# Order of VectorE's work inside one step of the eight-head attentions

## The chip, the cores and the metric

One core of one Trainium2 chip runs the whole program in a single launch. The metric is the device time of that core in microseconds; the kernel before took 3082.2 us (median of three runs, 3080.27 to 3089.55). The engines work from queues of their own, in the order in which the program gave them their instructions, and meet only at semaphores: TensorE (PE) multiplies, turns tiles (transposes) and fills the eight banks of PSUM, ScalarE (ACT) and VectorE (DVE) read these banks, GpSimd (POOL) works in SBUF, SyncE (SP) issues transfers.

## The reference, cut to what matters

1024 tokens of width 1024 pass two layers of a first kind and two of a second kind. A layer of the first kind projects its input, runs a differential attention of four heads with a bias by relative position, runs an attention of eight query heads on two key and value heads, and projects out. A layer of the second kind has a gating unit, an indexer that selects up to 256 keys for each query, and an attention of eight query heads on one key head over the selected, causal keys. The eight-head attentions, cut short:

```python
def gqa_attention(q, k, v):            # first kind: every key, 8 heads on 2
    sc = einsum('bgrqd,bgkd->bgrqk', qblk * d ** -0.5, kt)
    p = softmax(sc, axis=-1)
    return einsum('bgrqk,bgkd->bgrqd', p, vt)

def sparse_attention(...):             # second kind: 8 heads on 1, causal and selected
    sc = where(valid, einsum('bthd,btkd->bthk', qb, k_sel) * attn_scale, -inf)
    p = softmax(sc, axis=-1)
    return einsum('bthk,btkd->bthd', p, v_sel)
```

All of it is in float32. The kernel gets this accuracy from TensorE's faster format by cutting each operand of a product in two: a high part, which is the value rounded to that format, and a low part, which is the value less its high part. A product is then the sum of two or three products of such parts.

## The kernel before, in words

`heads_phase` computes one eight-head attention. It is called once per layer, four times in all: with the tag `b_` in the two layers of the first kind, and with the tag `x_` in the two layers of the second kind, where it is causal.

Its unit of work is a **row**: 128 queries of one head against their keys, a tile of 128 partitions by up to 1024 elements. There are 64 rows in a call, numbered g = 0 to 63: four pairs of heads, in each pair eight blocks of 128 queries, in each block first the one head and then the other. In the `b_` calls every row has 1024 keys. In the `x_` calls a row has 128 keys for the first block of queries, 256 for the second and so on up to 1024, and then the next pair of heads begins with 128 again; the selection comes in as the `bias` that is added.

The life of a row is: TensorE multiplies its scores into PSUM (`scores`, L1111, two rows at a time, in banks 0 to 3). VectorE adds the bias or zero, negates, writes the row to SBUF and keeps the maximum (`shift`, L970). ScalarE takes the exponential in place and keeps the sum (`exponent`, L906). VectorE takes the reciprocal of the sum (`invert`, L978). GpSimd scales the row by it (L1034). When four rows of one head are ready, TensorE turns them: a **turned tile** is 128 keys by 512 queries, made of up to four transposes (`turn`, L1072), in one of the banks 4 to 6. ScalarE copies the high part out (`take` of the scalar program, L890), VectorE the low part, which is the bank less the high part (`take` of the vector program, L953), and TensorE multiplies both by the values (`product`, L1089 and L1090). After the last tile of a group ScalarE reads the result (`close`, L897 and L900) and GpSimd gates it (L1006, L1011).

Every engine has its own program, and each program is a loop over the same steps g = START to END, here from -5 to 78. A table called `plan` says which tiles are turned in which step. In the `b_` calls it is two tiles in each of the steps 8 to 71; in the `x_` calls it is one or two, of 128 to 512 columns. The queries and keys of the next pair of heads are turned by the same table ("stack" tiles, L1066, L882, L945), one more tile in each of a few steps. What the engines issue in step g is this:

- TensorE: the products of the tiles of `plan[g-2]`; if g is odd, the scores of rows g+1 and g+2, which wait until row g has been shifted; then the turns of `plan[g]`.
- ScalarE: the high parts of `plan[g-1]`; every fourth step a `close`; then the exponential of row g, which waits for the shift of row g.
- VectorE: the shift of row g, which waits for its scores; the reciprocal of row g-1; then the low parts of `plan[g-1]`, each of which waits for its high part.
- GpSimd: the scaling of row g-1, and every fourth step two operations of 64 by 512.

Nothing reorders these queues: an instruction that waits holds up all that its engine was given later. In the `b_` calls the last steps of the four-head attention before it are interleaved with steps -5 to 14 (`next(before)`), so that this attention's rows overlap the end of the other one.

Of the kernel before, what the change touches and what calls it, by code (L numbers as in the profile page):

```python
# [721 lines left out]
def heads_phase(nc, env, tag, groups, queries, group_of, y_of, bias=None, load=(), ahead=(), gating=(), host=None):  # L722
# [13 lines left out]
    def query_tile(g):  # L736
        return g % (2 * T) // 2
# [13 lines left out]
    def group_with(g):  # L751
        return 2 * (g // 8) + g % 2
# [10 lines left out]
    def tile_lo(n, j):  # L763
        return max(0, j - QB * half_of(n)) * P if causal else 0
# [9 lines left out]
    plan = {g: [] for g in range(START, END + 1)}  # L774
    for z, (_, at) in enumerate(stacks):
        plan[at].append(("stack", z, 0))
        plan[at if at < 0 else at + 1].append(("stack", z, 1))
# [8 lines left out]
    last_tile = [number["attn", n, tiles(n) - 1] + 1 for n in range(NSB)]  # L786
    last_rank = [rank["attn", n, tiles(n) - 1] + 1 for n in range(NSB)]
    stack_of = {what: z for z, (what, _) in enumerate(stacks)}

    with ExitStack() as c:  # L790
# [36 lines left out]
        def stack(z):  # L827
            what, i = stacks[z][0]
            return key_st[i][:, :, :] if what == "k" else query_st[i % 2][:, :, :]

        def scale_of(z):
            return 1.0 if stacks[z][0][0] == "k" else HD ** -0.5

        def bank(e):
            return 4 + number[e] % (2 if host and number[e] < 4 else 3)

        def score_view(g):
            pair = 2 * (g % 2)
            kn = keys(g)
            if kn > BANK:  # L840
                return ps[:, pair:pair + 2, 0:kn // 2]
            return ps[:, pair, 0:kn]

        def row_view(row, g):
            kn = keys(g)
            return row.rearrange("p (b n) -> p b n", b=2) if kn > BANK else row

        def prob(g):
            return pr[g % RING]

        with Phase(nc, joins=host.ph if host else None, continued=True) as ph:
# [8 lines left out]
            @ph.sync  # L860
            def _(sp):
                if host:
                    sp.wait_ge(host.y_done, host.blocks)
                for dst, src in load:
                    sp.dma_start(dst, src).then_inc(y_in, 16)
                for dst, src, sem in ahead:
                    sp.dma_start(dst, src).then_inc(sem, 16)

            @ph.block.scalar
            def _(act):  # L870
                def take(e):
                    act.wait_ge(turned, number[e] + 1)
                    if e[0] == "stack":
                        _, z, side = e
                        what, p = stacks[z][0]
                        if what == "q" and p >= 2:
                            act.wait_ge(scored, T * (p - 1))
                        if host and z < 2:
                            act.wait_ge(host.shifted, 2 * (host.rows - T))
                        elif host:  # L880
                            act.wait_ge(host.pv_done, host.products)
                        nc.scalar.activation(stack(z)[:, 0, side * BANK:(side + 1) * BANK], ps[:, bank(e), :], ACT.Copy,  # L882
                                             scale=scale_of(z)).then_inc(stk_hi, 1)
                        return
                    kk, lo = rank[e], tile_lo(e[1], e[2])
                    if kk >= SLOTS:
                        act.wait_ge(pv_done, kk - SLOTS + 1)
                    elif host:
                        act.wait_ge(host.pv_done, host.products)
                    nc.scalar.activation(ath[:, kk % SLOTS, lo:], ps[:, bank(e), lo:], ACT.Copy).then_inc(th_done, 1)  # L890
# [47 lines left out]
            @ph.block.vector  # L938
            def _(dve):
                def take(e):  # L940
                    if e[0] == "stack":
                        _, z, side = e
                        cols = slice(side * BANK, (side + 1) * BANK)
                        dve.wait_ge(stk_hi, moved[e])
                        nc.vector.scalar_tensor_tensor(stack(z)[:, 1, cols], ps[:, bank(e), :], scale_of(z),  # L945
                                                       stack(z)[:, 0, cols].bitcast(F32), ALU.mult,
                                                       ALU.subtract).then_inc(stk_lo, 1)
                        return
                    kk, lo = rank[e], tile_lo(e[1], e[2])
                    dve.wait_ge(th_done, kk + 1)  # L950
                    if kk >= SLOTS:
                        dve.wait_ge(pv_done, kk - SLOTS + 1)
                    nc.vector.tensor_tensor(atl[:, kk % SLOTS, lo:], ps[:, bank(e), lo:],  # L953
                                            ath[:, kk % SLOTS, lo:].bitcast(F32), ALU.subtract).then_inc(tl_done, 1)

                def shift(g):
                    dve.wait_ge(scored, g // 2 + 1)
                    if g >= NS:
                        dve.wait_ge(exped, g - NS + 1)
                    if g >= RING:  # L960
                        dve.wait_ge(turned, last_tile[group_with(g - RING)])
                    elif host and g == 0:
                        dve.wait_ge(host.scored, host.rows)
                    elif host and g == 5:
                        dve.wait_ge(host.combined, host.rows)
                    elif host and g == 8:
                        dve.wait_ge(host.turned, host.turns)
                    added = (row_view(bias(query_tile(g)), g) if causal
                             else zero.unsqueeze(2).broadcast_to([P, 2, BANK]))
                    nc.vector.tensor_tensor_reduce(out=row_view(prob(g), g), in0=score_view(g), in1=added,  # L970
                                                   scale=-1.0, scalar=3.0e38, op0=ALU.add, op1=ALU.min,
                                                   accum_out=nm[:, g % NS:g % NS + 1]).then_inc(shifted, 1)

                def invert(g):
                    dve.wait_ge(exped, g + 1)
                    if g >= NS:
                        dve.wait_ge(normed, g - NS + 1)
                    nc.vector.reciprocal(rr[:, g % NS:g % NS + 1], sums[:, g % NS:g % NS + 1]).then_inc(recip, 1)  # L978

                before = steps[1](dve)  # L980
                if not causal:
                    nc.vector.memset(zero, 0.0).then_inc(zeroed, 1)
                    dve.wait_ge(zeroed, 1)
                for _ in range(alone):
                    next(before)
                for g in range(START, END + 1):
                    next(before, None)
                    if 0 <= g < NB:
                        shift(g)
                    if 1 <= g <= NB:  # L990
                        invert(g - 1)
                    for e in plan.get(g - 1, []):
                        take(e)
                    for i in range(NG):
                        if g == split_step[i]:
                            dve.wait_ge(v_hi, i + 1)
                            nc.vector.tensor_tensor(vv[i][:, :, HD:], groups[i][1],
                                                    vv[i][:, :, 0:HD].bitcast(F32), ALU.subtract).then_inc(v_lo, 1)
# [1687 lines left out]
```

## Time and profile before

| | before |
|---|---|
| median of three runs | 3082.2 us |
| the profiled execution | 3083.09 us |
| its span | 3081.2 us |
| its mean granted TensorE clock | 0.937 of full speed |
| PE / DVE / ACT / POOL busy | 2690.7 / 2030.6 / 1566.3 / 1155.1 us |

The page also cuts the span into 40 equal slices of about 77 us; a digit is the busy share of a slice in tenths. The first shift of the two `b_` calls starts at 542.5 and 1375.2 us of the span, that of the two `x_` calls at 2123.0 and 2812.6 us; the last one follows some 190 us later in a `b_` call and some 134 us later in an `x_` call. Below, times on the left of a timeline row are microseconds from the span's start.

### The profile page before, as it was taken

How to read it: one execution, taken by the hardware profiler on the slowest of the kernel's cores; microseconds unless marked ns; L12 is line 12 of the kernel's file. 1: busy time of each engine (PE TensorE's matmuls, PEld its weight loads, DVE VectorE, ACT ScalarE, POOL GpSimd, SP SyncE). 2: the span in 40 equal slices, each digit the busy share in tenths (PEclk: the TensorE clock that was granted, in tenths of full speed). 3: DMA queues.
4: the chain of work that ended last, by engine and by line, in shares of the span. 5: the costliest groups of instructions: out<-in, count | busy, mean ns of one | idle time of the engine just before them, and what ended most of it. 6: DMA issues, size and time to landing. Idle time of an engine off the chain costs nothing. (4 is left out here: it accounts for less than half of the span.)

```text
span 3081.2 us, 41522 instructions
## 1 busy us (share of the span) xinstructions
PE 2690.7 (87%) x14032; PEld 2114.1 (69%) x14032; DVE 2030.6 (66%) x4318; ACT 1566.3 (51%) x3035; POOL 1155.1 (37%) x981
## 2 busy tenths in 40 slices
PE   6999888898979997989989796997889697997887
PEld 5877666676868775656777585776667575776666
DVE  4472487798434724877974348997767358997766
ACT  3221276788423113757873216684764316684751
POOL 0100277564001003765630002984741002984731
PEclk9999899999989998999999899998999898998999
DMA  4443210101324421001022101110032100110022
GB/s 124 118 140 99 91 40 8 42 1 43 109 70 130 141 81 56 20 8 42 1 95 91 55 21 28 45 45 25 1 123 76 58 18 28 45 45 25 1 89 82
DMA packets 90750, 181.93 MB, mean 59 GB/s; under 512 B 12552, under 2 KB 27912, under 8 KB 90504
## 3 DMA queue, kind: packets, MB, share of 16 engines
q1 hardware_dynamic: 74124, 150.69, 15.4%
q10 hardware_dynamic: 16416, 28.61, 3.1%
q8 instruction: 111, 1.82, 0.3%
q14 instruction: 99, 0.81, 0.1%
HBM read 149.87 MB, written 33.33 MB: 59 GB/s over the span
## 5 line engine op out<-in xcount | busy, mean ns | idle before, releaser
L1362 POOL TENSOR_SCALAR a_prob<-a_prob,a_ratio 128x1024 f32<-128x1024 f32 x64 | 72.1, 1127 | 515.8 <-DVE a_ratio L1321 515.8
L718 PE MATMUL ps<-w_hi,hh 128*128 128x512 f32 (+1 forms) x640 | 242.4, 379 | 22.2 <-DVE w_lo L603 10.1
L718 PE MATMUL ps<-w_lo,hh 128*128 128x512 f32 (+1 forms) x640 | 240.0, 375 | 0.0
L718 PE MATMUL ps<-w_hi,hl 128*128 128x512 f32 (+1 forms) x640 | 239.9, 375 | 0.0
L1801 PE MATMUL ps<-o_w_hi,hh 128*128 128x512 f32 x512 | 212.5, 415 | 24.3 <-DVE o_w_lo L1725 24.3
L2263 DVE TENSOR_SCALAR_CACHE_REDUCE select_rows<-masks,select_cuts 128x1024 bf16<-128x1024 int16 (+7 forms) x264 | 230.2, 875 | 0.2
L1801 PE MATMUL ps<-o_w_lo,hh 128*128 128x512 f32 x512 | 207.6, 405 | 0.0
L1801 PE MATMUL ps<-o_w_hi,hl 128*128 128x512 f32 x512 | 206.7, 404 | 0.0
L1781 POOL TENSOR_TENSOR o_rstd<-o_rstd,nhalf 128x1 f32<-128x1 f32 x56 | 46.7, 835 | 409.6 <-DVE o_rstd L1662 235.3
L1034 POOL TENSOR_SCALAR b_prob<-b_prob,a_guest_small 128x1024 f32<-128x1024 f32 x128 | 144.6, 1129 | 127.6 <-DVE a_guest_small L978 124.9
L1310 DVE CUSTOM_DVE_ANT_0 a_prob<-ps,a_bias 128x1024 f32<-128x1024 f32 x128 | 151.7, 1222 | 59.5 <-PE ps L1452 55.0
L970 DVE CUSTOM_DVE_ANT_1 b_prob<-ps,a_guest_small 128x1024 f32<-128x1024 f32 x128 | 156.1, 1219 | 31.3 <-PE ps L1111 31.3
L953 DVE TENSOR_TENSOR a_attn_t_lo<-ps,a_attn_t_hi 128x512 fp32r<-128x512 f32 x256 | 163.7, 681 | 14.2 <-ACT a_attn_t_hi L890 13.7
L906 ACT ACTIVATE b_prob<-b_prob,a_guest_small 128x1024 f32<-128x1024 f32 x128 | 147.6, 1154 | 30.5 <-DVE a_guest_small L970 30.2
L2437 PE MATMUL ps<-hh,w_hi 128*128 128x512 f32 x384 | 153.7, 400 | 10.6 <-ACT y L2187 7.6
L890 ACT ACTIVATE a_attn_t_hi<-ps 128x512 fp32r<-128x512 f32 x256 | 139.4, 599 | 35.6 <-PE ps L1072 34.7
L718 PEld LDWEIGHTS ps<-w_hi,hh 128*128 128x128 f32 x640 | 121.7, 190 | 52.0 <-DVE w_lo L603 20.6
L539 ACT ACTIVATE w_hi<-w_raw 128x512 fp32r<-128x512 f32 (+1 forms) x56 | 33.7, 601 | 240.9 <-PE ps L718 229.4
L2079 PE MATMUL ps<-w_hi,hh 128*128 128x512 f32 (+1 forms) x384 | 140.0, 365 | 17.6 <-DVE w_lo L2047 12.6
L1265 ACT ACTIVATE a_prob<-a_prob,a_neg_max 128x1024 f32<-128x1024 f32 x128 | 146.0, 1148 | 17.8 <-DVE a_neg_max L1310 17.5
L1365 POOL TENSOR_TENSOR a_prob<-a_prob 128x1024 f32<-128x1024 f32 x64 | 152.7, 2386 | 5.3
L2437 PE MATMUL ps<-hl,w_hi 128*128 128x512 f32 x384 | 152.8, 398 | 0.0
(356 smaller groups left out, 7914.8 us busy)
## 6 DMA issues: line engine op xcount, KB each, us to landing
w_early<-in_w_in SPq DMA_DIRECT2D x108, 256.0 KB, 2.8
ada_w<-in_w_ada ACTq DMA_DIRECT2D x96, 256.0 KB, 2.7
w_raw<-in_w_in SPq DMA_DIRECT2D x84, 256.0 KB, 2.7
ak<-gates SPq DMA_DIRECT2D x32, 256.0 KB, 3.7
xcur<-aq SPq DMA_DIRECT2D x16, 512.0 KB, 3.6
y<-xcur SPq DMA_DIRECT2D x16, 512.0 KB, 3.8
a_bias<-bias_tiles SPq DMA_DIRECT2D x8, 960.0 KB, 4.9
bq<-in_w_out SPq DMA_DIRECT2D x12, 512.0 KB, 4.0
```

Source lines behind the costliest of these rows:

```text
L718: mm = nc.tensor.matmul(o, lhs, rhs, start=(k == 0 and i == 0), stop=(k == K - 1 and i == 2))
L906: nc.scalar.activation(prob(g), prob(g), ACT.Exp, bias=nm[:, g % NS:g % NS + 1], scale=-1.0, accum_out=sums[:, g % NS:g % NS + 1]).then_in ...
L953: nc.vector.tensor_tensor(atl[:, kk % SLOTS, lo:], ps[:, bank(e), lo:], ath[:, kk % SLOTS, lo:].bitcast(F32), ALU.subtract).then_inc(tl_do ...
L970: nc.vector.tensor_tensor_reduce(out=row_view(prob(g), g), in0=score_view(g), in1=added, scale=-1.0, scalar=3.0e38, op0=ALU.add, op1=ALU.m ...
L1034: nc.gpsimd.tensor_scalar(prob(b), prob(b), rr[:, b % NS:b % NS + 1], 0.5, ALU.mult, ALU.mult).then_inc(normed, 1)
L1265: nc.scalar.activation(row, row, ACT.Exp, bias=nm[:, g % NS, m:m + 1], scale=-1.0, accum_out=out).then_inc(exped, 1)
L1310: nc.vector.tensor_tensor_reduce(out=row, in0=scores_of(g, m), in1=bias, scale=-1.0, scalar=3.0e38, op0=ALU.add, op1=ALU.min, accum_out=nm ...
L1365: nc.gpsimd.tensor_tensor(row0(g), row0(g), row1(g), ALU.add).then_inc(combined, 1)
L1801: mm = nc.tensor.matmul(o, lhs, rhs, start=(k == 0 and i == 0), stop=(k == K - 1 and i == 2))
L2079: mm = nc.tensor.matmul(ps[:, b, 0:n], lhs, rhs, start=(k == 0 and i == 0), stop=(k == K - 1 and i == 2))
L2263: spare_free[z] = mark(nc.vector.tensor_scalar(spare[:, z, 0:(qb + 1) * P], values, against, None, op, ALU.add, accum_out=column(count_of, ...
L2437: mm = nc.tensor.matmul(ps[:, b, :], lhs, rhs, start=(k == 0 and i == 0), stop=(k == K - 1 and i == 2))
```

## The change

In each step of the loop of the vector program of `heads_phase`, the low parts of the turned tiles of `plan[g-1]` are issued before the shift of row g and the reciprocal of row g-1, and no longer behind them. No instruction is added, removed or resized, and the programs of the other engines stay as they are. It applies to all four calls.

```diff
@@ -985,12 +985,12 @@
                     next(before)
                 for g in range(START, END + 1):
                     next(before, None)
+                    for e in plan.get(g - 1, []):
+                        take(e)
                     if 0 <= g < NB:
                         shift(g)
                     if 1 <= g <= NB:
                         invert(g - 1)
-                    for e in plan.get(g - 1, []):
-                        take(e)
                     for i in range(NG):
                         if g == split_step[i]:
                             dve.wait_ge(v_hi, i + 1)
```

## Rows read from the trace of the kernel before

**Rows 1.** The page, part 1: engine, busy us, share, instructions.

```profile
PE 2690.7 (87%) x14032; PEld 2114.1 (69%) x14032; DVE 2030.6 (66%) x4318; ACT 1566.3 (51%) x3035; POOL 1155.1 (37%) x981
```

**Rows 2.** Windows: shift 8 to shift 63 of each call, busy us by engine, clock.

```profile
576.00:733.00 157.00, 152.18 (x1010) 116.42 (x1011) 141.02 (x283) 139.73 (x253) 97.19 (x87) 0.99 0.06 21
1408.70:1565.70 157.00, 152.33 (x1011) 116.51 (x1011) 141.08 (x284) 139.68 (x253) 97.35 (x87) 0.99 0.06 21
2133.90:2257.40 123.50, 104.88 (x665) 80.91 (x665) 89.50 (x250) 96.40 (x219) 93.36 (x96) 0.90 0.00 1
2823.50:2946.70 123.20, 104.57 (x665) 80.96 (x665) 89.61 (x249) 96.53 (x219) 93.30 (x96) 0.90 0.00 1
```

**Rows 3.** Waits of 576 to 733 us: us in total, times, longest.

```profile
DVE b_prob L970 <- PE ps L1111: 14.6, 27, 1.9
...
DVE a_attn_t_lo L953 <- ACT a_attn_t_hi L890: 1.1, 5, 0.2
```

**Rows 4.** Timeline, a few steps of a b_ call: start us, us, engine, line.

```profile
652.96 1.09 ACT L890 ACTIVATE a_attn_t_hi<-ps 128x512 fp32r<-128x512 f32 x2
...
653.59 1.29 DVE L953 TENSOR_TENSOR a_attn_t_lo<-ps,a_attn_t_hi 128x512 fp32r<-128x512 f32 x2 [0.21 <-ACT a_attn_t_hi L890]
...
653.93 1.16 ACT L906 ACTIVATE b_prob<-b_prob,a_guest_small 128x1024 f32<-128x1024 f32 x1
...
654.79 1.22 DVE L970 CUSTOM_DVE_ANT_1 b_prob<-ps,a_guest_small 128x1024 f32<-128x1024 f32 x1
...
655.06 1.09 ACT L890 ACTIVATE a_attn_t_hi<-ps 128x512 fp32r<-128x512 f32 x2
...
656.05 1.18 ACT L906 ACTIVATE b_prob<-b_prob,a_guest_small 128x1024 f32<-128x1024 f32 x1
...
656.07 1.66 PE L1111 MATMUL ps<-b_key_stack,b_query_stack 64*128 64x512 f32 x12 [0.16 <-DVE a_guest_small L970]
...
657.66 1.09 PE L1072 MATMUL ps<-ident,b_prob 128*128 128x128 f32 x8
...
658.36 1.09 ACT L890 ACTIVATE a_attn_t_hi<-ps 128x512 fp32r<-128x512 f32 x2 [1.04 <-PE ps L1072]
```

**Rows 5.** Windows of an x_ call around a fall of the clock.

```profile
2185.00:2190.00 5.00, 3.08 (x19) 2.07 (x19) 4.08 (x15) 4.19 (x11) 4.82 (x5) 0.87 0.01 2
2190.00:2195.00 5.00, 5.00 (x25) 4.56 (x24) 2.46 (x6) 3.86 (x8) 2.33 (x4) 0.50 0.01 3
```

**Rows 6.** Windows around one in a b_ call, the same columns.

```profile
570.00:575.00 5.00, 3.73 (x24) 2.87 (x24) 2.58 (x8) 3.43 (x6) 2.72 (x3) 0.92 0.00 0
575.00:580.00 5.00, 5.00 (x28) 3.46 (x26) 3.58 (x8) 2.73 (x6) 4.70 (x8) 0.74 0.00 0
```

**Rows 7.** Timeline, work of TensorE at the lower clock, and what follows it.

```profile
573.56 2.40 PE L1111 MATMUL ps<-b_key_stack,b_query_stack 64*128 64x512 f32 x12
...
576.00 1.23 DVE L970 CUSTOM_DVE_ANT_1 b_prob<-ps,a_guest_small 128x1024 f32<-128x1024 f32 x1 [1.90 <-PE ps L1111]
...
2189.47 1.94 PE L1072 MATMUL ps<-ident,x_prob 128*128 128x128 f32 x8 [0.51 <-DVE x_attn_t_lo L953]
...
2192.72 0.43 DVE L970 CUSTOM_DVE_ANT_0 x_prob<-ps,masks 128x256 f32<-128x256 f32 x1
```

**Rows 8.** Groups by line, 2133.9 to 2257.3 us: busy us, mean ns, idle.

```profile
L906 ACT ACTIVATE x_prob<-x_prob,x_neg_max 128x640 f32<-128x640 f32 (+7 forms) x55 | 43.9, 798 | 7.0 <-DVE x_neg_max L970 6.8
L970 DVE CUSTOM_DVE_ANT_0 x_prob<-ps,masks 128x640 f32<-128x640 f32 (+7 forms) x55 | 43.1, 783 | 15.2 <-PE ps L1111 15.2
L953 DVE TENSOR_TENSOR x_attn_t_lo<-ps,x_attn_t_hi 128x512 fp32r<-128x512 f32 (+1 forms) x78 | 41.1, 549 | 14.8 <-ACT x_attn_t_hi L890 14.2
L890 ACT ACTIVATE x_attn_t_hi<-ps 128x512 fp32r<-128x512 f32 (+1 forms) x78 | 35.8, 486 | 19.8 <-PE ps L1072 19.5
```

**Rows 9.** Timeline, scores of two narrow rows of an x_ call and what follows.

```profile
2191.66 1.01 PE L1111 MATMUL ps<-x_key_stack,x_query_stack 64*128 64x256 f32 x6
...
2192.60 0.69 PE L1072 MATMUL ps<-ident,x_prob 128*128 128x128 f32 x2
```

**Rows 10.** Timeline, scores of two wide rows of an x_ call and what follows.

```profile
2253.90 1.66 PE L1111 MATMUL ps<-x_key_stack,x_query_stack 64*128 64x512 f32 x12 [0.57 <-DVE x_neg_max L970]
2255.49 0.55 PE L1072 MATMUL ps<-ident,x_prob 128*128 128x128 f32 x3
```

## The prediction

> **What bounds the kernel now.** I read the engine totals first, then the four calls of `heads_phase` one by one. TensorE is busy 2690.7 of 3081.2 us [rows 1], so most of the kernel follows it, but inside the calls two or three engines are nearly full together. Between the shift of row 8 and that of row 63, a `b_` call takes 157.0 us: TensorE is busy 152.2, VectorE 141.0, ScalarE 139.7. An `x_` call takes 123.5 and 123.2 us, with TensorE at 105 and VectorE at 90 [rows 2]. These stretches are the ones that the change touches, 55 shifts each, with turned tiles in every step. The waits say what is late in a `b_` call: VectorE waits 14.6 us in 27 pieces for scores, which is once in two rows, and only 1.1 us for high parts [rows 3]. So VectorE runs shift, reciprocal, two low parts, and meets a high part that has almost always been copied. The timeline shows why that is so: while VectorE shifts row g (654.79), ScalarE has gone on from the exponential of the row before (653.93) to the two high copies (655.06), and the low parts come only after the shift. High copies and shift lie side by side. That is the slack to watch.
>
> **The change, part by part.** Nothing is added or taken away, so what has to be found is which waits get a new place. Write S(g) for the shift, E(g) for the exponential, H(g) for the high parts of the tiles of `plan[g-1]` and L(g) for their low parts. ScalarE issues H(g), E(g), H(g+1), E(g+1). VectorE issued S(g), L(g), S(g+1), L(g+1) and now issues L(g), S(g), L(g+1), S(g+1). As a cyclic order that looks the same, a low part between any two shifts, but it is another low part: L(g+1) now stands between S(g) and S(g+1), where L(g) stood. L(g+1) needs H(g+1). ScalarE has this behind E(g), and E(g) waits for S(g). So every row now closes a serial chain: S(g), E(g), H(g+1), L(g+1), S(g+1). Before, H(g+1) had the whole of S(g+1) as cover. Behind the waiting low part on VectorE stand the next shift and the reciprocal, behind these TensorE's next scores, ScalarE's next exponential and GpSimd's scaling, so no engine can run ahead of the ring.
>
> The price of one turn of this ring in a `b_` call, start to start [rows 4]: shift to exponential 654.79 to 656.05, 1.26; exponential to first high copy 653.93 to 655.06, 1.13; first high copy to first low part 652.96 to 653.59, 0.63 (VectorE had waited 0.21 for it, so that is the true delay); two low parts to the next shift 653.59 to 654.79, 1.20. Sum 4.22 us. This holds for a shift of odd g.
>
> For even g a second chain is longer, because the scores of row g are issued before the turns of `plan[g-1]` and wait for S(g-1): shift to scores 654.79 to 656.07, 1.28; scores to turns 656.07 to 657.66, 1.59; turns to high copy 657.66 to 658.36, 0.70; then again 0.63 and 1.20. Sum 5.40 us [rows 4]. Before, the scores alone stood between these two shifts and the turns were hidden.
>
> From shift 8 to shift 63 there are 28 links of the odd kind and 27 of the even kind: 28 x 4.22 = 118.2 and 27 x 5.40 = 145.8. Eight stack tiles fall in these steps, each with one more low part of about 0.60 (half of 1.20): 4.8. Together 268.8 us against 157.0 [rows 2], so **+112 us** per `b_` call with TensorE's clock unchanged.
>
> In an `x_` call the terms are the group means [rows 8]. Shift 0.783 and 0.05 until the next engine starts (as 1.22 stands to 1.26 and 1.28 in rows 4): 0.83. Exponential 0.82. High copy 0.486 + 0.03: 0.52. Low parts 0.549 less the 0.08 by which the next one overlaps, 0.47 each, with 78 tiles in 55 steps 1.42 of them: 0.67. An odd link is 2.84. An even link replaces the exponential by scores and turns. Wide scores take 1.59 from start to start [rows 10]; narrow ones took 0.94 at the lower clock [rows 9], say 0.54 at the full one; over the eight widths I take 1.00, and 0.62 for the turns, which are often fewer than four: 3.64. 28 x 2.84 + 27 x 3.64 = 177.8, and six stack tiles at 0.6 make 181.4, against 123.5 [rows 2]: **+58 us**.
>
> **The clock.** TensorE's work for two rows of a `b_` call is at most 152.2 / 27.5 = 5.5 us. In a ring of 4.22 + 5.40 = 9.6 us it has all of it ready early (turns and products follow the scores), so about 4.1 us in each 9.6 us are idle and in one piece. In the trace, 3.08 us of work in 5 us, in pieces, was followed by a granted clock of 0.50, which is 1.2 GHz; so it was, less deep, in the `b_` call at 575 us [rows 5, 6]. A stretch with TensorE nearly full kept 0.99 of 2.4 GHz [rows 2]. I expect the clock to fall in most of these idle pieces and to come back during the work behind them, and then it is the scores and the first turns that run at half speed, and these are on the ring. Priced: scores across part of a fall took 2.44 us (573.56 to 576.00), as against 1.59, and at most 2 x 1.59 = 3.18; I take 2.8. From the start of slow turns to the next shift it was 3.25 (2189.47 to 2192.72) as against 0.70 + 0.63 + 1.20 = 2.53 [rows 7]. An even link at the low clock is 1.28 + 2.8 + 3.25 = 7.33, which is 1.93 more. All 27 of them would add 52 us, none of them nothing. I take two thirds, +35. In the `x_` calls the scores are 1.00 and not 1.59, so the surcharge is some 1.2 us, 33 us for all; these calls are at 0.90 already and have less in one piece, so I take half, +16.
>
> On this the Trainium skill has a rule that speaks against me: TensorE: Matmul & The Clock Gate, section "Loop structure matters more than you think", says that a copy out of PSUM by VectorE between groups of matmuls does not cost TensorE its warm clock, and that it is long waits for transfers that do. Its example has the next matmuls follow at once. By it the surcharge of the paragraph above would be nothing. The trace at 2185 to 2195 us, with no transfer to wait for (DMA share 0.01), had the clock fall to 0.50, so here the row and the broad reading of the rule differ.
>
> **What is moved past.** The reciprocal of row g-1 now comes a low part later. GpSimd waits for it, but has 97 busy us in 157 [rows 2] and now 1.7 times the time; a group's first turn needs its last row two steps on. I cost it at nothing; if that cover were gone, it would be the 1.2 us of two low parts in one step of four. The low parts of the last rows are issued no earlier than before, so the tails behind shift 63 and the steps below 9, which have no tiles of this phase but stacks ahead of row 0, cost nothing either. No DMA is moved, and no queue of SP or GpSimd.
>
> **Sum.** A `b_` call: 112 + 35 = +147. An `x_` call: 58 + 16 = +74. Two of each: +442. The profiled execution took 3083.1, 0.9 above the median of 3082.2, so both give some **3525 us**, 14% more.
>
> **The rivals.**
> - The clock stays at 2.4 GHz in the rings. Only 2 x (112 + 58) = +340: 3422 us. For it speaks that `b_` calls hold 0.99 today; against it the idle of 4.1 us in one piece.
> - The clock is low in every even link: 2 x (112 + 52 + 58 + 33) = +510, 3592 us. For it: the idle piece repeats at every second row. Against: the work behind it is long enough that the clock rises again, and a late, slow piece of work makes the next idle piece shorter.
> - The other side, faster. If ScalarE had the high parts ready when VectorE starts a step, the low parts would fill VectorE's wait for scores (14.6 us in a `b_` call, 15.2 in an `x_` call [rows 3, 8]) and free banks and products a step earlier; at best 2 x (14.6 + 15.2) = -60, 3023 us. It decides if H(g) is issued ahead of the wait for S(g-1) on ScalarE. It is not: the code puts E(g-1), which waits for that shift, in front of it.
> - The change does less than it says: the ring binds only for even g, as if the odd one were hidden in work that the ring leaves over. A row takes 157.0 / 55 = 2.85 us today. Then per `b_` call 27 x (5.40 - 2.85) = 69, and in proportion (58 / 112) 36 per `x_` call: +210, 3293 us. But an odd link of 4.22 is above 2.85 too, and its four terms wait for each other, so nothing can hide it.
>
> **How the numbers follow.** The forecast (some even links slow) gets 0.55, the low clock everywhere 0.25, the full clock 0.14, the half ring 0.03, the faster case with no change 0.03. The range goes from the full clock to the low clock with 5 us per call for waits that my sums leave out: 3420 to 3610; what is left out is the half ring and the other side, and a little of each end. Apart from no change one can tell about 0.3%, 9 us; every slower case is far beyond: slower 0.97, same 0.02, faster 0.01.
>
> **What would show it.** In the changed kernel, VectorE should wait for high parts (L953 on L890) instead of for scores, in nearly every step: some 2 us each time, (269 - 141) / 55 = 2.3 in a `b_` call. In a timeline the order should be shift, exponential, high copies, low parts, shift with no overlap, 4.2 us from an even row to the odd one and 5.4 to 7.3 from an odd row to the even one. ScalarE's and VectorE's busy times must not move. The clock of a `b_` call should be below 0.99, near 0.8. If VectorE's waits for high parts stay near 1 us per call, my reading of ScalarE's order is wrong; if the clock is 0.99 and the time near 3422, only the surcharge is.

## The result

| | before | changed |
|---|---|---|
| median | 3085.9 us (3080.3 to 3091.2, 4 runs) | 3546.4 us (3533.7 to 3549.8, 4 runs) |
| ratio, with its 95% interval | | 1.149 [1.146, 1.152] |
| span of the profiled execution | 3081.2 us | 3532.0 us |
| mean granted TensorE clock | 0.937 | 0.891 |

The change made the kernel 460 us slower; 3525 had been forecast.

The page of the changed kernel, part 1, engine, busy us, share and instructions:

```profile
PE 2822.2 (80%) x14032; PEld 2218.5 (63%) x14032; DVE 2035.5 (58%) x4318; ACT 1584.6 (45%) x3035; POOL 1151.5 (33%) x981
```

Against [rows 1], VectorE's and ScalarE's work has hardly moved (+5 and +18 us). TensorE has gained 132 busy us with the same instructions: part of them run at the lower clock. The windows of the changed kernel from shift 8 to shift 63 of its four calls, columns as in [rows 2] (start and end, length, busy us of TensorE, its weight loads, VectorE, ScalarE and GpSimd, then clock, DMA share and GB/s):

```profile
574.70:884.40 309.70, 201.95 (x1023) 154.83 (x1023) 145.50 (x285) 146.98 (x256) 97.14 (x87) 0.80 0.03 11
1557.70:1867.50 309.80, 201.99 (x1022) 154.75 (x1023) 145.48 (x285) 146.97 (x256) 97.20 (x87) 0.80 0.03 11
2434.50:2634.70 200.20, 129.06 (x668) 100.64 (x668) 88.76 (x250) 100.77 (x221) 95.02 (x97) 0.76 0.00 1
3197.70:3398.50 200.80, 126.53 (x668) 98.96 (x668) 88.52 (x250) 100.56 (x221) 95.00 (x97) 0.76 0.00 1
```

157.0 us have become 309.7 and 309.8, and 123.5 and 123.2 have become 200.2 and 200.8: 460 us in these four stretches, against 451 in the span. The other 9 us were gained back outside them and were not traced further. (The profiled execution was the fastest of the four; the medians differ by 460 us.) The clock fell from 0.99 to 0.80 and from 0.90 to 0.76. Waits of the first stretch, us in total, times, longest, against [rows 3]:

```profile
DVE a_attn_t_lo L953 <- ACT a_attn_t_hi L890: 143.6, 60, 4.6
PE ps L1111 <- DVE a_guest_small L970: 106.5, 27, 4.5
...
ACT b_prob L906 <- DVE a_guest_small L970: 94.6, 55, 2.5
ACT a_attn_t_hi L890 <- PE ps L1072: 60.9, 39, 2.8
...
DVE b_prob L970 <- PE ps L1111: 1.9, 1, 1.9
```

VectorE's wait for high parts went from 1.1 to 143.6 us. Its shifts wait 1.9 us for scores, no longer 14.6: the scores are now ready, because VectorE is late. One turn of the chain in the changed kernel's timeline, start and duration in us:

```profile
769.08 1.22 DVE L970 CUSTOM_DVE_ANT_1 b_prob<-ps,a_guest_small 128x1024 f32<-128x1024 f32 x1
...
770.34 1.15 ACT L906 ACTIVATE b_prob<-b_prob,a_guest_small 128x1024 f32<-128x1024 f32 x1 [1.90 <-DVE a_guest_small L970]
...
771.49 1.06 ACT L890 ACTIVATE a_attn_t_hi<-ps 128x512 fp32r<-128x512 f32 x2
772.09 1.29 DVE L953 TENSOR_TENSOR a_attn_t_lo<-ps,a_attn_t_hi 128x512 fp32r<-128x512 f32 x2 [1.72 <-ACT a_attn_t_hi L890]
773.30 1.22 DVE L970 CUSTOM_DVE_ANT_1 b_prob<-ps,a_guest_small 128x1024 f32<-128x1024 f32 x1
...
774.58 2.93 PE L1111 MATMUL ps<-b_key_stack,b_query_stack 64*128 64x512 f32 x12 [4.05 <-DVE a_guest_small L970]
...
777.44 1.21 PE L1072 MATMUL ps<-ident,b_prob 128*128 128x128 f32 x8
778.25 1.09 ACT L890 ACTIVATE a_attn_t_hi<-ps 128x512 fp32r<-128x512 f32 x2 [2.45 <-PE ps L1072]
...
778.88 1.29 DVE L953 TENSOR_TENSOR a_attn_t_lo<-ps,a_attn_t_hi 128x512 fp32r<-128x512 f32 x2 [4.28 <-ACT a_attn_t_hi L890]
...
780.09 1.21 DVE L970 CUSTOM_DVE_ANT_1 b_prob<-ps,a_guest_small 128x1024 f32<-128x1024 f32 x1
```

Each step of this path starts when the one before it lets it: shift, exponential, high parts, low parts, shift takes 4.22 us (769.08 to 773.30). Then shift, scores, turns, high, low, shift takes 6.79 us; TensorE had stood idle for 4.05 us, and its scores take 2.86 (774.58 to 777.44) and not 1.59.

### The profile page after: what moved, and what is told of

Its sections match the earlier page's. It is cut to its first block and busy times, and to the rows that moved or that the text cites. A ratio compares the mean times of both kernels' runs of the same rounds, so it can differ in the third digit from the quotient of the medians.

```text
span 3532.0 us, 41522 instructions
## 1 busy us (share of the span) xinstructions
PE 2822.2 (80%) x14032; PEld 2218.5 (63%) x14032; DVE 2035.5 (58%) x4318; ACT 1584.6 (45%) x3035; POOL 1151.5 (33%) x981
## 3 DMA queue, kind: packets, MB, share of 16 engines
q8 instruction: 111, 1.82, 0.2%
## 5 line engine op out<-in xcount | busy, mean ns | idle before, releaser
L1111 PE MATMUL ps<-b_key_stack,b_query_stack 64*128 64x512 f32 x768 | 159.7, 569 | 217.3 <-DVE a_guest_small L970 217.3
L1111 PEld LDWEIGHTS ps<-b_key_stack,b_query_stack 64*128 64x128 f32 x768 | 99.0, 266 | 262.3 <-DVE a_guest_small L970 216.6
L718 PE MATMUL ps<-w_hi,hh 128*128 128x512 f32 (+1 forms) x640 | 242.7, 379 | 22.2 <-DVE w_lo L603 10.1
L953 DVE TENSOR_TENSOR x_attn_t_lo<-ps,x_attn_t_hi 128x512 fp32r<-128x512 f32 x192 | 102.5, 555 | 208.8 <-ACT x_attn_t_hi L890 208.4
L1111 PE MATMUL ps<-x_key_stack,x_query_stack 64*128 64x512 f32 (+4 forms) x576 | 99.4, 486 | 151.3 <-DVE x_neg_max L970 148.4
L1034 POOL TENSOR_SCALAR x_prob<-x_prob,x_recip 128x256 f32<-128x256 f32 (+7 forms) x128 | 95.4, 746 | 271.5 <-DVE x_recip L978 271.1
L1111 PEld LDWEIGHTS ps<-x_key_stack,x_query_stack 64*128 64x128 f32 x576 | 66.5, 262 | 174.9 <-DVE x_neg_max L970 143.1
L1072 PEld LDWEIGHTS ps<-ident,b_prob 128*128 128x128 f32 x1024 | 145.0, 168 | 48.6 <-issue 34.9
L1072 PE MATMUL ps<-ident,b_prob 128*128 128x128 f32 x1024 | 169.8, 319 | 6.6 <-DVE a_attn_t_lo L953 3.5
```

The costliest lines, as they stand in the source:

```text
L718: mm = nc.tensor.matmul(o, lhs, rhs, start=(k == 0 and i == 0), stop=(k == K - 1 and i == 2))
L1034: nc.gpsimd.tensor_scalar(prob(b), prob(b), rr[:, b % NS:b % NS + 1], 0.5, ALU.mult, ALU.mult).then_inc(normed, 1)
L1072: mm = nc.tensor.transpose(ps[:, bank(e), i * P:(i + 1) * P], prob(rows_in(n)[i])[:, j * P:(j + 1) * P], ident[:, :])
L1111: mm = nc.tensor.matmul(ps[:, 2 * m + b, 0:w], q_st[rows, qe, tok], k_st[rows, ke, cols], start=(i == 0), stop=(i == 2))
```

## The experiments

"Odd link" is the time from the start of an even shift to the next, odd one; "even link" from an odd shift to the even one behind it. Spans of calls run from shift 8 to shift 63. Each ratio is to runs of the kernel before on the same chip (medians 3080 to 3084 us).

**x_calls_only.** The change in the `x_` calls alone.

```diff
+                    for e in lows if causal else []: take(e)
                     shift(g); invert(g - 1)
+                    for e in [] if causal else lows: take(e)
```

> The new order in the two x_ calls alone; the b_ calls keep the old one. If each call pays for its own serial chain and nothing passes between them, the two x_ calls grow by 77 us each, as in the changed kernel, and the b_ calls stay at 157 us from shift 8 to shift 63: 3086 + 154 = 3240 us, within 10. If part of the loss of the changed kernel came from elsewhere (the clock carried over, a later start of the next phase), the two parts would not add up and this kernel would lie over 20 us away from 3240.

Measured 3236.3 us, 1.051 [1.047, 1.054]. The first `b_` call takes 157.0 us as before, the `x_` calls 200.9 and 202.3. Each call pays for itself and the parts add up.

**warm_filler.** The changed kernel with work for TensorE in its idle pieces.

```diff
+ if not causal and g % 2 and 11 <= g < NB:   # PE, ahead of the scores
+     for i in range(24): transpose(bank of the next turn, ident, ident)
```

> The changed kernel, with 24 transposes of the identity added in each odd step of the b_ calls, into a bank that the next turns overwrite, in the idle piece of TensorE ahead of the scores (24 x 0.11 = 2.6 us at the full clock, idle piece about 4.1 us). If the low clock is what makes an odd-to-even link 6.9 us and not 5.40, the clock stays near 1.0 in the b_ calls, these links fall to 5.4 and the odd ones stay at 4.22: 309.7 - 40 = 270 us a call, 3546 - 80 = 3466 us. If the 5.40 was simply too low and the clock costs nothing, the links stay at 6.9 and the time at 3546, or goes above it by what the filler delays.

Measured 3478.3 us, 1.129 [1.124, 1.134]; the `b_` calls take 278.1 and 275.7 us, the `x_` calls, which have no filler, 202.3 and 200.7. Window of the first `b_` call, and a piece of its timeline (the filler is L1123, the added line has moved the others by one):

```profile
570.20:848.30 278.10, 231.58 (x1667) 196.65 (x1668) 143.99 (x285) 145.30 (x256) 97.89 (x87) 0.97 0.04 12
```

```profile
702.35 1.22 DVE L971 CUSTOM_DVE_ANT_1 b_prob<-ps,a_guest_small 128x1024 f32<-128x1024 f32 x1
...
703.63 1.66 PE L1112 MATMUL ps<-b_key_stack,b_query_stack 64*128 64x512 f32 x12 [1.60 <-DVE a_guest_small L971]
...
705.22 1.09 PE L1073 MATMUL ps<-ident,b_prob 128*128 128x128 f32 x8
705.91 1.09 ACT L891 ACTIVATE a_attn_t_hi<-ps 128x512 fp32r<-128x512 f32 x2 [1.05 <-PE ps L1073]
...
707.75 1.22 DVE L971 CUSTOM_DVE_ANT_1 b_prob<-ps,a_guest_small 128x1024 f32<-128x1024 f32 x1
...
708.88 2.78 PE L1123 MATMUL ps<-ident 128*128 128x128 f32 x24
```

With useless work in the gap the clock is 0.97, and the even link is 5.40 (702.35 to 707.75), the sum of the prediction to the hundredth; 22 of the 27 even links of this call lie between 5.38 and 5.49. More work for TensorE made the kernel 68 us faster by the medians, and the two `b_` calls together 66. They are 8 and 6 us above the 270 expected: five even links of the first call take 6.4 to 9.0, one of them before the filler begins and two with scores that start only 3.38 us after the shift, behind the filler.

**exp_behind_high.** The changed kernel, ScalarE's exponential one step later.

```diff
-                    if 0 <= g < NB: exponent(g)
+                    if 1 <= g <= NB: exponent(g - 1)
```

> The changed kernel, with ScalarE's exponential of a row one step later, so behind the high parts of that step: H(g), E(g-1), H(g+1), E(g). If the odd link of 4.22 is the chain shift, exponential, high part, low part, the exponential now leaves it: the link falls to what VectorE needs, 1.20 + 0.08 + 1.22, 2.5 to 2.9 us; the even link keeps scores and turns, 5.4 at the full clock and up to 7.3. A b_ call 28 x 2.6 + 27 x 5.4 to 6.9 + 5 = 224 to 264, an x_ call about 150 to 170: 3270 to 3390 us. If ScalarE's order is not on the path (the loss is the late reciprocal, or VectorE's own order), nothing changes: 3546 us.

Measured 3324.2 us, 1.079 [1.075, 1.083]; calls 235.7, 236.2, 163.8, 165.7 us. An odd link and the even link behind it:

```profile
702.70 1.22 DVE L970 CUSTOM_DVE_ANT_1 b_prob<-ps,a_guest_small 128x1024 f32<-128x1024 f32 x1
...
703.92 1.27 DVE L953 TENSOR_TENSOR a_attn_t_lo<-ps,a_attn_t_hi 128x512 fp32r<-128x512 f32 x2
...
705.10 1.22 DVE L970 CUSTOM_DVE_ANT_1 b_prob<-ps,a_guest_small 128x1024 f32<-128x1024 f32 x1
...
706.38 1.66 PE L1111 MATMUL ps<-b_key_stack,b_query_stack 64*128 64x512 f32 x12 [2.06 <-DVE a_guest_small L970]
...
710.50 1.22 DVE L970 CUSTOM_DVE_ANT_1 b_prob<-ps,a_guest_small 128x1024 f32<-128x1024 f32 x1
```

Odd links fall from 4.22 to 2.40, which is VectorE's own work. Even links in a `b_` call are 5.4 at least (705.10 to 710.50) and 6.1 in the mean, with the clock at 0.90. So the exponential is on the odd link and not on the even one.

**turns_before_scores.** The changed kernel, TensorE's turns of an odd step ahead of its scores.

```diff
+                    if g % 2: turns of plan[g]
                     if g % 2: scores(g + 1)
-                    turns of plan[g]
+                    if g % 2 == 0: turns of plan[g]
```

> The changed kernel, with TensorE's turns of an odd step ahead of the scores of that step. If the even link is shift, scores, turns, high part, low part, the turns leave it and the chain through the exponential is left for both kinds: 55 x 4.22 + 5 = 237 us for a b_ call, and here the low clock costs little (shift 1.28 and slow scores 2.8 to 2.93 are 4.2 together, as long as the other chain). An x_ call 55 x 2.84 + 4 = 160. 3086 + 2 x (80 + 37) = 3320 us, 3300 to 3350. If the turns are not on the path, 3546.

Measured 3347.6 us, 1.087 [1.084, 1.090]; calls 244.0, 242.2, 171.0, 168.0 us. Even links go from 6.98 in the mean to between 4.22 and 4.38 in 23 of 27 steps, and most odd ones stay at 4.22. What is left on an even link is the chain through the exponential:

```profile
704.35 1.22 DVE L970 CUSTOM_DVE_ANT_1 b_prob<-ps,a_guest_small 128x1024 f32<-128x1024 f32 x1
...
705.61 1.15 ACT L906 ACTIVATE b_prob<-b_prob,a_guest_small 128x1024 f32<-128x1024 f32 x1 [0.92 <-DVE a_guest_small L970]
...
706.88 1.09 ACT L890 ACTIVATE a_attn_t_hi<-ps 128x512 fp32r<-128x512 f32 x2
...
707.51 1.29 DVE L953 TENSOR_TENSOR a_attn_t_lo<-ps,a_attn_t_hi 128x512 fp32r<-128x512 f32 x2 [1.86 <-ACT a_attn_t_hi L890]
...
708.71 1.21 DVE L970 CUSTOM_DVE_ANT_1 b_prob<-ps,a_guest_small 128x1024 f32<-128x1024 f32 x1
```

The time lies at the upper end of what was expected: the `x_` calls take 8 to 11 us more than the 160 that the group means gave, and a few steps with a third tile take up to 7.6.

**one_low_first.** Half of the change: of two low parts the first ahead of the shift.

```diff
+                    for e in lows[:len(lows) // 2]: take(e)
                     shift(g); invert(g - 1)
+                    for e in lows[len(lows) // 2:]: take(e)
```

> The new order for half of the tiles only: in a step with two turned tiles the first low part stands ahead of the shift and the second behind; a single tile is taken behind, as before. If the terms of the chain add up, a b_ call's links are each one low part (0.60) shorter than in the changed kernel: 3.62 and 6.3 (6.9 with the clock's part, less 0.60), 28 x 3.62 + 27 x 6.3 + 3 = 274 us. An x_ call has two tiles in half of its steps: about 160. 3086 + 2 x (117 + 37) = 3390 us, 3360 to 3420. If only the number of low parts ahead of the shift counted, half of the loss: 3316.

Measured 3307.6 us, 1.072 [1.069, 1.074]: 82 us below what was expected, outside its range, and near the 3316 of the other reading, half of the loss. The total can't tell the two apart; the links do. Odd links are 3.62 and the shortest even ones 4.80, each 0.60 less than with two, as expected. What failed is, for some 47 us, the clock's part: I had kept all of it (6.3), and the mean is 5.5 in the `b_` calls, 250.3 and 250.9 us. Window of the first:

```profile
572.20:822.40 250.20, 183.87 (x1018) 135.59 (x1018) 142.46 (x284) 146.62 (x256) 97.75 (x87) 0.89 0.04 13
```

A shorter link leaves a shorter idle piece, and the clock is 0.89 instead of 0.80. The other 36 us are the `x_` calls, in which single tiles have no ring here: 142.0 and 141.6 us, not 160.

**reciprocal_last.** The kernel before, with the reciprocal behind the low parts.

```diff
                     shift(g)
+                    low parts of plan[g - 1]
                     invert(g - 1)
-                    low parts of plan[g - 1]
```

> The kernel before, with the reciprocal of the last row behind the low parts and not between shift and low parts: shift, low parts, reciprocal. It is the only other thing that the change delays. GpSimd has 60 us of idle time in a b_ call of 157, and a group's first turn needs its last row two steps on, so I expect no difference: 3086 us, within 9. If the reciprocal's place matters (GpSimd's scaling would come 1.2 us later in each row and delay the turns of every fourth step), up to 27 x 1.2 / 2 = 16 us a call, 3150 us.

Measured 3093.9 us, 1.0025 [1.0015, 1.0035], some 8 us: small, but not nothing. Two low parts of the kernel before, behind an odd and an even shift (those of [rows 4]), with the reciprocal in front:

```profile
655.93 0.16 DVE L978 RECIPROCAL a_guest_small<-a_guest_small 128x1 f32<-128x1 f32 x1
656.01 1.27 DVE L953 TENSOR_TENSOR a_attn_t_lo<-ps,a_attn_t_hi 128x512 fp32r<-128x512 f32 x2
...
658.93 0.16 DVE L978 RECIPROCAL a_guest_small<-a_guest_small 128x1 f32<-128x1 f32 x1
659.00 1.27 DVE L953 TENSOR_TENSOR a_attn_t_lo<-ps,a_attn_t_hi 128x512 fp32r<-128x512 f32 x2
```

And in this kernel, an odd shift at 655.73 and the even one behind it:

```profile
655.73 1.21 DVE L970 CUSTOM_DVE_ANT_1 b_prob<-ps,a_guest_small 128x1024 f32<-128x1024 f32 x1
...
656.86 1.28 DVE L953 TENSOR_TENSOR a_attn_t_lo<-ps,a_attn_t_hi 128x512 fp32r<-128x512 f32 x2
...
659.29 1.09 ACT L890 ACTIVATE a_attn_t_hi<-ps 128x512 fp32r<-128x512 f32 x2 [1.05 <-PE ps L1072]
...
659.92 1.29 DVE L953 TENSOR_TENSOR a_attn_t_lo<-ps,a_attn_t_hi 128x512 fp32r<-128x512 f32 x2
...
661.13 0.15 DVE L978 RECIPROCAL a_guest_small<-a_guest_small 128x1 f32<-128x1 f32 x1
661.20 1.21 DVE L970 CUSTOM_DVE_ANT_1 b_prob<-ps,a_guest_small 128x1024 f32<-128x1024 f32 x1
```

The reciprocal takes 0.07 to 0.09 us of VectorE wherever it stands: behind an odd shift the low part starts 1.13 us after the shift without it and 1.22 with it. There VectorE waits for the next scores anyway. Behind an even shift the low part comes some 0.63 after its high part in both kernels (658.36 to 659.00, 659.29 to 659.92). So in the kernel before the reciprocal was hidden in that short wait, and behind the low parts it is not. That is 0.07 us more in a step where VectorE is the bound; the four calls are 0.8, 0.8, 1.6 and 0.4 us longer. The rest of the difference lies outside these stretches and is open.

**both_rings_open.** exp_behind_high and turns_before_scores together.

> The changed kernel with both of these edits, the exponential behind the high parts and the turns ahead of the scores. If the two serial chains are the whole loss, both are open now: between an odd and an even shift stand shift to scores and scores, 1.28 + 1.7 = 3.0 us, with two low parts (1.2) beside them, between an even and an odd one VectorE's own 2.5. That is the kernel before, within a per cent: 3060 to 3110 us. If there is a third cost in the new order, for instance the later reciprocal, it stays above 3110.

Measured 3160.3 us, 1.024 [1.023, 1.026]; calls 184.0, 183.9, 137.7, 138.1 us. Opening both chains took away 386 us of the 460. That two serial chains were the whole loss was wrong, or my edits brought a cost of their own. The timeline of this kernel:

```profile
717.31 1.21 DVE L970 CUSTOM_DVE_ANT_1 b_prob<-ps,a_guest_small 128x1024 f32<-128x1024 f32 x1
...
718.59 1.66 PE L1111 MATMUL ps<-b_key_stack,b_query_stack 64*128 64x512 f32 x12 [0.92 <-DVE a_guest_small L970]
...
720.17 0.51 PE L1089 MATMUL ps<-a_attn_t_hi,b_values 128*128 128x512 f32 x1
...
721.21 1.03 PE L1072 MATMUL ps<-ident,b_prob 128*128 128x128 f32 x8
...
721.85 1.09 ACT L890 ACTIVATE a_attn_t_hi<-ps 128x512 fp32r<-128x512 f32 x2 [2.04 <-PE ps L1072]
...
722.48 1.29 DVE L953 TENSOR_TENSOR a_attn_t_lo<-ps,a_attn_t_hi 128x512 fp32r<-128x512 f32 x2 [0.89 <-ACT a_attn_t_hi L890]
...
723.68 1.21 DVE L970 CUSTOM_DVE_ANT_1 b_prob<-ps,a_guest_small 128x1024 f32<-128x1024 f32 x1
```

A third chain is to be read in it, over two rows: odd shift, scores, products, turns, high parts, low parts, next odd shift, 6.37 us, where two rows took 5.7 before. And the waits of the first `b_` call have one that the kernel before does not have in this stretch:

```profile
DVE a_guest_small L978 <- ACT b_prob L906: 9.4, 13, 0.8
```

In every fourth step ScalarE's exponential now stands behind the two copies of a `close`, and VectorE's reciprocal, ahead of the low parts, waits for it. That is a cost of the first edit and not of the change; how much of the 27 us of a `b_` call it makes was not tried by itself.

**third_ring_open.** The same, with the turns of an even step ahead of its products.

> both_rings_open was 3160 us and not 3060 to 3110, with 184 us in a b_ call. Its timeline shows a third chain, over two rows: shift (odd), scores 1.28, products 1.58, turns 1.04, high part 0.64, low part 0.63, next but one shift 1.20, together 6.37 us, 27.5 times that is 175. This kernel puts the turns of an even step ahead of the products of that step, which takes 1.04 out: 5.33, less than the 5.4 to 5.7 of the kernel before. If that chain is the third cost, a b_ call falls to 150 to 165 us and the time to 3075 to 3120. If the cost is the exponential that now stands behind the two copies of a close, nothing much changes: 3160 us.

Measured 3174.9 us, 1.031 [1.029, 1.033]; the `b_` calls 183.7 us both. The expectation failed: ScalarE's high copies waited 30.0 us for turns in the first `b_` call of both_rings_open and wait 30.3 for products here. No gain in the `b_` calls is also what the other reading, the exponential behind a `close`, had forecast. The four stretches together are 3 us shorter; that the kernel is 15 us longer comes from outside them and was not traced.

**fifth_slot.** third_ring_open with five instead of four buffers for high and low parts in the `x_` calls.

> third_ring_open did not get faster (3175 us): its ScalarE waits 29.8 us in a b_ call and 15.5 us in an x_ call for products (L1090) instead of turns. A high copy goes into one of four buffers and needs the product of the tile four places before, so turning the order of turns and products round only swapped one wait for the other. This kernel gives the x_ calls a fifth buffer (in the b_ calls there is no room). If the four buffers are what holds the chain, the waits for L1090 in an x_ call go to about nothing and the call gets 4 to 10 us shorter: 3155 to 3167 us. If they are only the name on a wait that turns would cause anyway, 3175.

Measured 3174.9 us, 1.029 [1.027, 1.032]. ScalarE's wait for products in the first `x_` call fell from 15.5 to 3.7 us, and its wait for turns grew from 15.4 to 23.1; the calls take 135.7 and 138.8 us, as against 137.9 and 135.2. So in the `x_` calls the buffers were mostly the name on the wait. In the `b_` calls a fifth buffer was not tried, and this is open.

**low_part_moved.** both_rings_open, with the last low part of an odd step back behind the shift.

> The same, and in odd steps the last low part goes behind the shift, so that three low parts (1.9 us) stand in the place where VectorE waits for scores and one in the other. If VectorE's wait of 0.5 us in two rows is all that is left to gain and TensorE does not become the bound, 27 x 0.5 = 13 us in each b_ call and somewhat less in an x_ call: up to 50 us below both_rings_open. If TensorE is the bound by then (5.2 to 5.5 us of work for two rows of 5.55), or the later products hold it up, there is no gain.

Measured 3150.5 us, 1.020 [1.018, 1.021]: 10 us below both_rings_open and still slower than the kernel before. Its `b_` calls gained 6 and 8 us of the 13 that were expected at most, its `x_` calls nothing.

**scores_first** and **one_low_held.** From the kernel before: TensorE's scores ahead of its products in odd steps; and the same with one low part of each even step held back behind the odd shift.

```diff
+                    if g % 2: scores(g + 1)
                     products of plan[g - 2]
-                    if g % 2: scores(g + 1)
```

> The kernel before with TensorE's edit of one_low_held alone: scores ahead of the products in odd steps. TensorE waits some 0.2 us for the odd shift today, so the products that stood in front of the scores were cover and come behind them now: the turns follow 1.0 us later, high parts too. If the turns have slack, 3086 us within 9; if not, up to 27 x 1.0 a call, 3190.

> From the kernel before: VectorE's 0.5 us of waiting for scores between an odd and an even shift is to be filled by a low part that is held back from the step before it (two low parts behind the odd shift become three, two behind the even one become one), and TensorE takes the scores ahead of the products in odd steps, since one of these products now comes later. No low part is ahead of a shift that its high part waits for, so no ring. If VectorE's wait is what is left, two rows go from 5.55 to 5.1 to 5.3 us: 3086 - 4 x 8 = 3055, 3040 to 3075. If TensorE's own work (5.2 to 5.5 us for two rows) or the three banks of turned tiles are the bound, 3086 or up to 3120.

Measured 3232.7 us, 1.049 [1.047, 1.050], and 3195.7 us, 1.036 [1.034, 1.038]. The first lies beyond the bad end that I gave, the second far beyond its own. The `b_` calls take 211 and 214 us, and 196 both. In scores_first odd links mostly take 3.4 us, the 1.0 more that was expected, but 5.3 and more where a `close` falls in them. Two rows tell why: a `close` of ScalarE needs the last product, which now comes behind the scores, and the exponential stands behind the `close`:

```profile
701.69 0.59 ACT L897 ACTIVATE b_o_hi<-ps 64x512 f32<-64x512 f32 x1 [2.25 <-PE ps L1090]
...
702.92 1.15 ACT L906 ACTIVATE b_prob<-b_prob,a_guest_small 128x1024 f32<-128x1024 f32 x1
```

No kernel tried here beats the one before.

## Why the prediction was right

- **The ring.** "ScalarE has this behind E(g), and E(g) waits for S(g)" is the cause of the odd link, and it is shown by exp_behind_high: with that order turned round the odd link falls by 1.82 us. The predicted 4.22 was measured as 4.22.
- **The even link.** The predicted 5.40 at the full clock was measured as 5.40 in warm_filler and exp_behind_high; that the turns are on it is shown by turns_before_scores. One low part is worth 0.60 in either link (one_low_first).
- **The clock.** Forecast: falls in most idle pieces, +35 us a call. In the changed kernel the mean even link of a `b_` call is 6.98, the slow ones 7.38 as against the 7.33 worked out. The size is right, but not the picture behind it: not two thirds of the links are slow and the rest at 5.40. In 26 of 27 the scores or the first turns take longer than at the full clock, in most of them only one of the two for its whole length, and the least of all links is 5.99. The excess is some 40 us a call, near the 35 because the partly slow links average out. warm_filler, with 32 and 34 us less in a call, shows that the idle pieces cause it. The Trainium skill (TensorE: Matmul & The Clock Gate, "Loop structure matters more than you think") can be read broadly, as no loss where the waits are for VectorE's copies; the trace does not agree with that reading (0.80 with the idle pieces, 0.97 with them filled).
- **The sums.** A `b_` call +153 (forecast +147), an `x_` call +77 and +78 (forecast +74). The largest error of an `x_` term is the odd link, 3.04 in the mean against 2.84: group means over widths put too little on it, since the even steps that feed it have the wider tiles.
- **The reciprocal at nothing.** Its place is worth some 8 us when the low parts are put between it and the shift (reciprocal_last). The change leaves it directly behind the shift, where VectorE then waits for high parts in any case, so this cost does not arise in it.
- **The rivals.** The full clock everywhere (3422) and the half ring (3293) are out by the links. The low clock everywhere (3592) is half right: it is low in nearly every even link, but in most of them not for the whole of the work that the link waits for. The faster case is out too: with the high parts issued ahead of the exponential, in exp_behind_high and both_rings_open, the kernel is still slower than before.

Luck has a part in the last digits: the shares of slow links, two thirds and one half, were choices. What stays open is the last 77 us of both_rings_open, which holds two more edits than the change; part of it is the wait for the exponential behind a `close` that one of these edits brought.

## What to carry to other kernels

A cyclic order can look unchanged while each operation meets a later partner: write the order of both queues side by side, with step numbers, and look for a loop of waits that passes through both. Here the sum of the starts around each loop was the new period, 4.22 and 5.40 us, while VectorE was busy less than half of the time. Before reordering one engine's step, check what the step of its supplier has in front of the operand; the slack of the kernel before lay in one engine working a step ahead of the other.

## What the runs showed of the hardware

Identity transposes with no use to the result (24 of them, 2.78 us in each 9.6) held the granted clock at 0.97, as against 0.80 without them, and took 68 us off the kernel. The same 12 scores took 1.59 us from start to start at 2.4 GHz and 2.86 behind an idle piece of 4.05 us. And a reciprocal that the profile lists with 0.16 us moves VectorE's next operation by 0.07 to 0.09; in the kernel before this was hidden in VectorE's short wait for the next high part, so taking it away from there gained nothing, and its new place had a price.
